# Dealing the modulation sums of layer 1 over four passes, moving norm rows away from their stores, and giving outputs banks of their own

## What is computed

```python
def _rmsnorm(h, g):
    hf = h * lax.rsqrt(jnp.mean(h * h, axis=-1, keepdims=True) + NORM_EPS)
    return hf * g

def _ffn_sublayer(h, mod, g_pre, g_post, w_in, w_out):
    shift, scale, gate = mod
    u = _rmsnorm(h, g_pre) * (1 + scale) + shift
    a, b = jnp.split(u @ w_in, 2, axis=-1)
    y = (jax.nn.silu(a) * b) @ w_out
    return h + 0.5 * gate * _rmsnorm(y, g_post)

# per layer i: nine modulation rows for each stream
mx = (silu(c)     @ ada_w[i] + ada_b[i]).reshape(9, 1024)
mc = (silu(c_ctx) @ ada_w[i] + ada_b[i]).reshape(9, 1024)
```

## Time and profile before

| what | us |
|---|---|
| median of 3 runs | 2854.84 (2852.12, 2854.84, 2856.62) |
| the profiled execution, by itself | 2847.95 |
| its span, first to last instruction | 2846.2 |
| TensorE busy | 2757.5 (97%) |
| VectorE busy | 2053.7 (72%) |
| ScalarE busy | 1607.9 (56%) |
| GpSimd busy | 138.7 (5%) |
| read from HBM | 559.17 MB, 197 GB/s over the span |

### The profile page before, as it was taken

The page is one execution under the profiler, slowest core; times in us unless marked ns, Lnnn a source line. Parts: engine busy times, 40 slices in busy tenths (PEclk is TensorE's granted clock), DMA queues, the critical chain, the costliest instruction groups (busy, mean ns, idle before and its releaser), DMA issues.

```text
span 2846.2 us, 37779 instructions
## 1 busy us (share of the span) xinstructions
PE 2757.5 (97%) x14816; PEld 2329.6 (82%) x14816; DVE 2053.7 (72%) x2655; ACT 1607.9 (56%) x2431; POOL 138.7 (5%) x140
## 2 busy tenths in 40 slices
PE   6999999989999999999999999999899999998999
PEld 5888888768888888888887788887688888896887
DVE  7879887777888898886536565665666565696664
ACT  5455555676555555555646654554855454476553
POOL 0000000000000000000040000000000000194000
PEclk9999999999999999999999999999999999999999
DMA  8667784206677787985552355554355565440553
GB/s 339 217 236 272 243 256 169 105 27 238 224 274 252 219 298 265 296 252 192 178 208 98 125 194 196 195 190 166 133 201 192 178 207 193 176 168 11 210 184 132
DMA packets 100561, 562.72 MB, mean 198 GB/s; under 512 B 20256, under 2 KB 20768, under 8 KB 43936
## 3 DMA queue, kind: packets, MB, share of 16 engines
q1 hardware_dynamic: 100384, 560.30, 56.8%
HBM read 559.17 MB, written 1.09 MB: 197 GB/s over the span
## 4 chain that ended last, share of the span: by engine, by line
PE 72%; DVE 10%; ACT 5%; issue 5%; DMA 4%; POOL 3%; SPq 0%; DVEq 0%; ACTq 0%; POOLq 0%
PE banks L867 19%; PE banks L873 10%; PE banks L368 9%; PE banks L369 9%; PE banks L1041 7%; PE banks L373 3%; PE banks L375 3%; PE banks L374 3%; DVE ada_terms L449 3%; DVE w_rest L352 3%; ACT w_high L342 2%; POOL od_glu L2374 2%; PE banks L841 2%; POOL normed L2370 1%; DMA w_raw<-in_w_ffn_in 1%
## 5 line engine op out<-in xcount | busy, mean ns | idle before, releaser
L352 DVE TENSOR_TENSOR w_rest<-w_raw,w_high 128x2048 fp32r<-128x2048 f32 x426 | 975.2, 2291 | 495.4 <-ACT w_high L342 494.5
L342 ACT ACTIVATE w_high<-w_raw 128x2048 fp32r<-128x2048 f32 x426 | 811.1, 1908 | 336.3 <-PE banks L1041 161.8
L867 PE MATMUL banks<-u_parts,w_high 128*128 128x512 f32 x3200 | 764.3, 391 | 2.2 <-DVE post_term L557 2.2
L867 PEld LDWEIGHTS banks<-u_parts,w_high 128*128 128x128 f32 x3200 | 588.2, 188 | 116.9 <-issue 2.5
L873 PEld LDWEIGHTS banks<-u_parts,w_rest 128*128 128x128 f32 x3200 | 410.2, 191 | 16.6 <-DVE w_rest L352 1.1
L873 PE MATMUL banks<-u_parts,w_rest 128*128 128x256 f32 x3200 | 415.2, 283 | 0.6 <-DVE w_rest L352 0.6
L368 PE MATMUL banks<-w_high,gated_high 128*128 128x512 f32 x968 | 378.9, 391 | 1.7 <-DVE gated L947 1.7
L369 PE MATMUL banks<-w_high,gated_rest 128*128 128x512 f32 x968 | 377.5, 390 | 0.0
L449 DVE CUSTOM_DVE_ANT_0 ada_terms<-ada_tiles,cond_rows 128x1024 f32<-128x1024 f32 x224 | 273.7, 1222 | 12.0 <-DMA ada_tiles<-in_w_ada 6.9
L1041 PE MATMUL banks<-w_rest,gated_high 128*128 128x512 f32 x968 | 258.9, 389 | 0.1
L368 PEld LDWEIGHTS banks<-w_high,gated_high 128*128 128x128 f32 x968 | 182.3, 188 | 39.3 <-issue 2.1
(11 more groups left out here) (307 smaller groups left out, 3334.6 us busy)
## 6 DMA issues: line engine op xcount, KB each, us to landing
w_raw<-in_w_ffn_in SPq DMA_DIRECT2D x242, 1024.0 KB, 5.0
w_raw<-in_w_ffn_out SPq DMA_DIRECT2D x121, 1024.0 KB, 5.0
ada_tiles<-in_w_ada SPq DMA_DIRECT2D x128, 512.0 KB, 5.0
w_raw<-in_w_mix SPq DMA_DIRECT2D x54, 1024.0 KB, 5.0
w_raw<-in_w_mix_out SPq DMA_DIRECT2D x22, 1024.0 KB, 4.9
ada_first<-in_w_ada SPq DMA_DIRECT2D x7, 1024.0 KB, 14.9
post_gain_row<-post_mod SPq DMA_DIRECT2D x10, 512.0 KB, 5.9
na_bias<-in_na_bias SPq DMA_DIRECT2D x1, 4096.0 KB, 14.1
```

Source lines behind the costliest of these rows:

```text
L342: act.activation(w_high(g)[:, 0:n], raw[:, g % RING, 0:n], ACT.Copy).then_inc(w_hi_ready, 1)
L352: nc.vector.tensor_tensor(w_rest(g)[:, 0:n], raw[:, g % RING, 0:n], w_high(g)[:, 0:n].bitcast(F32), ALU.subtract).then_inc(w_lo_ready, 1)
L867: pe.matmul(ps[n].rearrange("p (a n) -> p a n", a=2), hi[:, w], u[:, c, :, kt], start=kt == 0, stop=False)
```

## The change

**The deal of the sums (`ada_plan`).** Layer 1's 80 units (and m = 8 of layer 0) were dealt from in2x + 2 on to every even slot of an input half and to every slot of an output half, and ended at out3x + 9; now f = 0 of each input half and j = 1, 2, 4 and 6 of each output half get none, and the deal ends at out3c + 5. The two-tile slots, 16 before and after, were in3x + 10 to out3x + 9 and are out3x + 8 to 10, ten slots of in3c, and out3c + 0, 3 and 5. The stores go with the sums: s = 3 from slot out2c + 4 to in3x + 3, s = 4 from out3x + 0 to in3c + 8, s = 5 from in3c + 4 to v4x + 0; s = 2 stays at out2x + 0.

**VectorE's order (`ffn_dve`).** At f = 0 of a pass beside another stream, the scales of the last outputs come ahead of the next rest and not behind it. In an output half, a slot's sums come behind its norm step and not ahead.

**SyncE's order.** Gain rows come first between two slots, not behind the tiles and the store. A gain row whose turn was set by its store comes two slots behind it: that is (2, 0), from out2x + 0 to out2x + 2, and (0, 0), from out0x + 8 to out0x + 10. (1, 1) keeps its slot, in2x + 2, and goes ahead of the condition rows and three tiles there.

**Banks.** The outputs of (2, 0) to (3, 1) go to banks 6, 7 and 4, 5 (before 6, 7 and 2, 3), and all these passes share the order of gate banks that (2, 0) alone had. Of the exposed feed-forwards, s = 5, 8 and 11 put the second token tile into banks 1 and 3 (before 2 and 3), and s = 6 and 9 keep theirs and get other gate banks. With that no outputs share a bank with the last gates, and TensorE's wait for `in_summed` ahead of the second token tile is gone from `ffn_out_pe`.

```diff
--- before.py
+++ after.py
@@ -130,8 +130,10 @@
     spots = []
     for s in (2, 3):
         for c in "xc":
-            spots += [first[f"in{s}{c}"] + 2 * f for f in range(NF)] + [first[f"out{s}{c}"] + j for j in range(NF)]
-    tiles += [(g, *u) for g, us in zip(spots[1:], units) for u in us]
+            spots += [first[f"in{s}{c}"] + 2 * f for f in range(1, NF)]
+            spots += [first[f"out{s}{c}"] + j for j in range(NF) if j not in (1, 2, 4, 6)]
+    assert len(units) <= len(spots), (len(units), len(spots))
+    tiles += [(g, *u) for g, us in zip(spots, units) for u in us]
     return tiles
 
 
@@ -508,8 +510,10 @@
 
 
         def y_pair(s, c, tt):
-            return pairs[{(1, 0): [0, 1], (1, 1): [3, 2], (4, 0): [0, 1], (7, 0): [0, 1], (10, 0): [3, 2]}
-                         .get((s, c), [2, 1] if exposed(s) else [3, 1])[tt]]
+            if exposed(s) and s in FFNS and not behind_ffn(s):
+                return banks[:, 1:4:2] if tt else pairs[2]
+            return pairs[{(0, 0): [3, 1], (0, 1): [3, 1], (1, 0): [0, 1], (4, 0): [0, 1], (6, 0): [2, 1], (7, 0): [0, 1],
+                          (9, 0): [2, 1]}.get((s, c), [3, 2])[tt]]
 
         def u_pair(s, c, tt):
             if s >= 5:
@@ -758,8 +762,12 @@
 
 
 
+        def behind_ffn(s):
+
+            return s - 1 in FFNS
+
         def in_bank(s, f, tt):
-            return tt + 2 * (f % 2) if not exposed(s) else 2 * tt + f % 2
+            return tt + 2 * (f % 2) if not exposed(s) or behind_ffn(s) else 2 * tt + f % 2
 
         def gate_in(s, c, f, tt):
 
@@ -790,10 +798,12 @@
         def gate_banks(s, c, f):
 
             if exposed(s):
+                if behind_ffn(s):
+                    return ([6, 7, 0, 1], [4, 5, 2, 3])[f % 2]
                 return ([6, 7, 0, 2], [4, 5, 1, 3])[f % 2]
-            if (s, c) == (2, 0):
-                return ([0, 1, 2, 3], [4, 5, 6, 7])[f % 2]
-            return ([0, 1, 4, 5], [2, 3, 6, 7])[f % 2]
+            if s == 0:
+                return ([0, 1, 4, 5], [2, 3, 6, 7])[f % 2]
+            return ([0, 1, 2, 3], [4, 5, 6, 7])[f % 2]
 
         def gates_before(s, c):
 
@@ -1069,11 +1079,8 @@
                     if p and not exposed(s):
                         pe.wait_ge(y_taken, 4 * p)
                     pe.wait_ge(gate_done, b0 + 2 * NF - 2)
-                if k == 0 and tt == 1:
-                    if by_token(s, c, NF - 1):
-                        pe.wait_ge(gate_done, b0 + 2 * NF)
-                    elif exposed(s) or (s, c) == (2, 0):
-                        pe.wait_ge(in_summed, sums_before(s, c, NF))
+                if k == 0 and tt == 1 and by_token(s, c, NF - 1):
+                    pe.wait_ge(gate_done, b0 + 2 * NF)
                 if k % 2 == 0 and tt == 0:
                     pe.wait_ge(glo_done, b0 // 2 + k // 2 + 1)
 
@@ -1177,9 +1184,10 @@
             if (s, c) == (0, 0):
                 first_gates_dve()
             for f in range(3 if (s, c) == (0, 0) else 0, NF):
+                if f == 0 and not exposed(s):
+                    post_scales(*ends_beside(s, c), 1)
                 rests(g0 + 2 * f + LEAD)
                 if f == 0 and not exposed(s):
-                    post_scales(*ends_beside(s, c), 1)
                     post_add(*ends_beside(s, c), 1)
                 sums_at(g0 + 2 * f)
                 if (s, c) == (0, 0) and f < len(FIRST_CTX):
@@ -1197,7 +1205,6 @@
                 rests(split_upto(s, c, j))
                 if j == 0:
                     glo_dve(s, c, NF - 1)
-                sums_at(g1 + j)
                 if not exposed(s):
                     o = starts_beside(s, c)
                     if j == 1:
@@ -1208,6 +1215,7 @@
                         stat_dve(*o, 1)
                     if j == 6:
                         part_dve(*o, 1)
+                sums_at(g1 + j)
 
 
 
@@ -2848,11 +2856,13 @@
             gain_spots[s, 0] = first[f"in{s}x"] + 3
         gain_after = {}
         for (s, c), g in gain_spots.items():
-            gain_after.setdefault(max(g + AHEAD, store_spot.get(s, 0)), []).append((s, c))
+            gain_after.setdefault(max(g + AHEAD, store_spot.get(s, -2) + 2), []).append((s, c))
         pre_gain_after = {gain_spots[s - 1, 0] + AHEAD: s for s in range(6, 12)}
         mixer_after = {first["in0c"] + 4: 1, first["v4x"] + AHEAD: 4, first["in7"] + AHEAD - 1: 7, first["in10"] + AHEAD: 10}
 
         def between_slots(sp, g):
+            for s, c in gain_after.get(g, []):
+                load_post_gain(sp, s, c)
             if g == first["in2x"] + 2:
                 sp.wait_ge(mixers[1].sem["o_turned"], KT)
                 load_cond(sp, 0)
@@ -2861,8 +2871,6 @@
                 load_ada(sp, n)
             if g in store_after:
                 store_post_mod(sp, store_after[g])
-            for s, c in gain_after.get(g, []):
-                load_post_gain(sp, s, c)
             if g in pre_gain_after:
                 load_pre_gain(sp, pre_gain_after[g])
             if g in mixer_after:
```

## The result

The changed kernel took 2838.85 us in the median of 4 runs (2836.42 to 2839.3), the kernel before beside it 2855.73 us (4 runs, 2852.12 to 2859.28): ratio 0.9943, 95% interval 0.9931 to 0.9955. The profiled execution took 2836.42 us with a span of 2834.6, against 2847.95 and 2846.2 before: 11.5 us less. The trace gives about what the sum gave, in part by luck, and the medians of that set give more. In the last of the sets further down one execution of the kernel before took 7063.22 us; it is a slow one and stands in no ratio, median or count of this document.

What follows compares the result with a forecast made beforehand. The prediction took TensorE to carry the span, with other queues worth only the TensorE time they give back. Five terms summed to 10.88 us, taking the median from 2854.84 to 2843.9 us, range 2840 to 2852.

Steps and rivals of the forecast that it cites:

- The five terms: Excess over TensorE's floors: in0c 1.12, out0c 0.45, in2x 2.46, out2x 2.02, out3x 4.83 us, all to be won.
- Part 1: Head of a pass: scales ahead of the next weight split remove in0c's stall, 1.12 us.
- Part 4: Out2x: outputs sharing no bank with the gates remove the 1.75 us stall released by L947; 2.02 us gained.
- the whole effect into part 4, whose stall it feeds: In2x's end: the late weight slot behind the store, ACT waiting 5.97 us, was counted within out2x's 2.02 us.
- Parts 2 and 3 of out3x: Out3x: sums behind norm steps and the new deal remove the transposes' 2.97 us wait; 4.83 us gained.
- with half of that the stall would still be under 0.5: Out3x: the norm comes 5.1 us earlier against a 2.97 us wait, so half would suffice; 4.83 us gained.
- Covers: In3c: VectorE's load rises from 85.40 to 109.8 of 122.44 us, at a cost of zero.
- parts 1 and 2: Scales ahead of the split (in0c, 1.12 us); sums behind norm steps with the new deal (out0c 0.45, out3x 4.83 us).
- The fourth rival: Two-tile slots: each second tile late by 1.15 us, 18.4 us at 16 slots, giving 2862.3 us; chance 0.08.
- The third rival: Start of mixer 4: the moved store of s = 5 starves it, price 0.98 us, 2844.9 us; no chance of its own.
- the first case: Whole kernel: the full sum comes, around 2843.9 us, chance 0.64.
- the saving is the same in both, and the forecast for a median is 2854.84 - 10.9: Last step, whole kernel: the saving applied to the earlier runs' median as to the profiled execution, giving 2843.9 us.

Runs made afterwards that it cites:

- order_alone: Kernel before with only VectorE's two order changes (scales ahead of the rest at f = 0, sums behind the norm step): ratio 1.0005.
- gain_rows_alone: Kernel before with only the gain rows ahead of condition rows and tiles, and two slots behind their stores: ratio 0.9981.
- banks_alone: Kernel before with only the new banks and without TensorE's wait for the gate sum: ratio 0.9995.
- deal_alone: Kernel before with only the new deal of the sums: ratio 0.9983.
- after_again: Changed kernel run once more without edit, in the second set: 2835.74 us, ratio to the kernel before 0.9965.
- after_third: Changed kernel run once more without edit, in the next set: 2838.31 us, ratio to the kernel before 0.9966.
- store1_later: Changed kernel with the store of s = 1 four slots later: ratio to the kernel before 0.9959.
- best_try: Changed kernel with the store of s = 1 four slots later, old banks, and layer 0's sums ahead of norm steps: 2833.59 us, ratio to before 0.9949.
- before_again: Kernel before run once more without edit, in the second set: ratio 1.0003.

## Why the prediction was right, and where it was wrong

**The five terms.** In0c, in2x, out2x and out3x reached the floors named, out0c nearly: 10.3 us in the repeated pair against 10.88. As a sum read from floors it held. As an account of which part of the change gives which term it did not hold in three places.

- Part 1's 1.12 us: VectorE's new order cures in0c (order_alone 122.44; its two edits were not tried apart), but so do the gain rows alone. It has two cures, and I named one.
- Part 4's 2.02 us: the step "the whole effect into part 4, whose stall it feeds" put the gain on the wrong edit. The row to go by was ScalarE's 5.97 us, a cause, and not L947, the last link of its chain. The profile's releaser names who came last; gain_rows_alone and banks_alone show who was late.
- Parts 2 and 3 of out3x: the wait of 2.97 us does go with the order (0.88 left), as reckoned, but the 4.83 us don't go with it. The step "with half of that the stall would still be under 0.5" looked at one wait and not at the tiles and slots that are late in the rest of that half, which show next at w_rest. And some 1.5 of the 4.83 us were clock. The deal is what removes the waits.

**Covers.** In3c at 104.90 us of VectorE's time has no wait in the kernel after, as put; in gain_rows_alone its head, with 1.2 us to spare, did cost 1.66 us. In deal_alone and order_alone, each with one half of parts 1 and 2, in3c has 122.64 and 122.68 us and no wait. So the cover was thin, and parts 1 and 2 are what keeps it. The fourth rival's mechanism (second tiles late) did not occur: two waits, 2.6 us in all, none of them passed on.

**The third rival** I had at a small chance and inside the first case. Moving the store of s = 5 cost nothing: mixer 4 starts in 23.54 to 23.62 us in every trace. The store of s = 1, which stays where it was, is the one that starves a mixer. The profiled execution of after had this dearer than before (27.73 against 25.44: 1.1 us more of wait, and the lower clock behind it), and a wait of 1.07 us in out0x that after_again and after_third don't have. That one has the same cause, at the store of s = 0: the weight slot issued behind it at 190.79 landed after 16.0 us, and in after_again the like slot after 13.8. ScalarE waited 3.86 us for it, to 206.77, and the rests of this slot and the next were begun at 208.72 and 213.34, in after_again at 206.57 and 211.19. In order_alone, which has this wait as well, the slot was held by the gain row. My sum had it that the slots behind a store cost nothing; by these waits they can. The Trainium skill, "DMA: Bandwidth & Descriptors", section "Rules for kernel authors", has it that a transfer with a last dimension that isn't contiguous takes one descriptor per element, and that DMAs from all issuing engines run on the same 16 DMA engines. The rows agree as to the consequence that the prediction drew from it, slots that stay late with the gain row away from the store: in the kernel after the first slots behind the stores of s = 1, 2, 3 and 4 (issued at 387.97, 776.34, 1042.76 and 1255.03) landed after 14.0, 13.6, 12.2 and 13.6 us. Only the first of these four cost TensorE anything.

**The step that failed** is the last of the sum: "the saving is the same in both, and the forecast for a median is 2854.84 - 10.9". What was mis-sized is the level of 2854.84, not the 10.9: the medians lie 16.9 us apart in that set and 10.2 and 9.1 us in the next two. By the profiled executions the forecast would have been 2837.1, and the profiled execution of after took 2836.42. I took the three runs' median as the level and their scatter (2852.12 to 2856.62) as all the doubt about it, though the fourth number at hand, 2847.95, lay 4.2 us below the lowest of them. Three later sets put the kernel before at medians of 2845.98, 2847.38 and 2849.61, and of 73 later executions of it none is above 2853.3. So the level of 2854.84 to 2855.73 was the unusual figure, and the kernel after, at 2838.85 in the first set and 2835.74 and 2838.31 later, was not. What raised the kernel before in the first set is open: no trace of those runs exists, and the profiled one shows nothing of it. The chip and chance in four executions can't be told apart; a slower chip by itself would have raised the kernel after as well. A range that took that 7 us between one execution and the median in on the lower side would have gone to 2837 and held the time.

**Part of the 11.5 us between the two profiled executions is not the change either.** That 2836.42 came out near 2837.1 is partly luck. Behind mixer 4, which nothing touches, the head of in5x took 28.52 us in the kernel before and 25.59 us after. Here is TensorE's stretch in the kernel before, then the same in after_again, store1_later and best_try:

```profile
1603.42:1631.94 28.52, 26.61 (x108) 21.54 (x109) 14.77 (x20) 17.21 (x34) 0.00 (x0) 0.88 0.31 107
```

```profile
1592.49:1619.71 27.22, 25.22 (x109) 20.34 (x109) 14.76 (x20) 17.18 (x34) 0.00 (x0) 0.94 0.32 113
```

```profile
1591.70:1620.23 28.53, 26.62 (x109) 21.53 (x109) 14.79 (x20) 17.20 (x34) 0.00 (x0) 0.88 0.31 106
```

```profile
1590.37:1615.99 25.62, 23.57 (x108) 19.18 (x109) 14.69 (x20) 17.20 (x34) 0.00 (x0) 1.00 0.33 116
```

The same work with the same wait ahead, at a granted clock of 0.88, 0.94, 0.88 and 1.00. So of the 11.5 us some 2.9 are the clock at this place, 1.7 came behind it, with mixer 10 at a granted clock of 0.89 in the 30 us from 2472 before and 0.94 in the 30 us from 2463 after, and 6.93 are the start of mixer 4 (1414.47 to 1407.54): 10.8 from the five terms, less what out0x, mixer 1 and out3c lost.

## What to carry to other kernels

A stretch that runs at its floor elsewhere in the same trace gives the size of a gain well, but the releaser on the last wait does not give its cause: follow it to the first queue that fell behind, here SyncE held by a gain row behind a small scattered store. Parts of a change that take away successive waits can't be priced one by one. Alone they gave ratios of 1.0005, 0.9981, 0.9995 and 0.9983, which happen to add up to what all give together (0.36% against 0.35), but up to mixer 4 they come to 5.0 us in the traces (-2.1, 3.9, -0.4 and 3.5 against before_again) where all together give 9.95, each figure with a microsecond or two of clock in it: time won alone was waited away at the next late thing, one wait had two cures, and another moved from the norm to the weights when the order changed and went only with the deal. And a forecast of a median needs a range for the level of the kernel before, as wide as the distance of any execution that is at hand.

## What the runs showed of the hardware

- A store of 8 KB in pieces of four bytes makes the loads behind it late: the weight slot behind it landed after 14.0 us where the median is 5.1, and SyncE took 2.98 us to issue it, where 0.33 us is usual. The slots behind three later stores (8, 8 and 4 KB) landed after 12.2 to 13.6 us though they went out about 5 us after the store and with a usual issue, and cost TensorE nothing, where the store just ahead of mixer 1 cost 2 to 4 us.
- A wait of TensorE of about 3 us can be followed by the lower clock and need not be. Out3x has the granted clock at 0.97 behind waits of 2.97 and 2.80 us (the kernel before, before_again) and at 1.00 behind 2.88 and 3.43 us (gain_rows_alone, banks_alone). The loss is about 1.5 us each time, so a stretch's length compares only at like clock.
- The granted clock behind one and the same TensorE wait of 1.91 us differs from execution to execution. Kernel before, and kernel after, at the head of in5x:

```profile
1603.42 0.52 PE L831 MATMUL banks<-w_high_lead,u_parts 128*128 128x512 f32 x1 [1.91 <-ACT u_parts L693]
1603.74 0.63 PE L832 MATMUL banks<-w_rest_lead,u_parts 128*128 128x512 f32 x1
```

```profile
1596.46 0.47 PE L841 MATMUL banks<-w_high_lead,u_parts 128*128 128x512 f32 x1 [1.91 <-ACT u_parts L697]
1596.76 0.40 PE L842 MATMUL banks<-w_rest_lead,u_parts 128*128 128x512 f32 x1
```

- The matmul of 128x512 takes 0.63 us in the one and 0.40 in the other. Over a whole execution it shows in the mean granted clock: of the 73 later executions of the kernel before, those at 0.993 have a median of 2849.7 us (13), those at 0.996 one of 2844.7 (18). So some 5 us of the 10 over which one kernel's times scatter within a set go with the clock; inside each of the two groups the times still lie over 7 us, and no trace says what the rest is. The whole scatter is about as large as what this change gained.
